# Middle down group as merged units: seven products for tiles 0 and 1 with tile 2's plain products, weight sums on GpSimd

## The chip, the cores and the metric

The kernel runs on one core of a Trainium2 chip. The metric is device time in microseconds; the run takes one execution of the program, from inputs in HBM to outputs in HBM. Everything is float32; the matmuls take float32 operands that were split into a high part (written as fp32r) and a low part, with three passes per product (high x high, high x low, low x high).

## The reference

One inference step of a hybrid decoder layer on 1024 prompt tokens and 8 sample tokens (1032 columns): RMSNorm, an input projection, three parallel head groups (sliding window attention, a gated linear recurrence, a short convolution), an output projection, and a feed-forward part. The change touches the last of these:

```python
up = rmsnorm(x, g_ffn) @ w_up
upc, ffn_buf_new = causal_conv(ffn_buf, up, ffn_conv_w)
u, gt = jnp.split(upc, 2, axis=-1)
x = x + (jax.nn.silu(gt) * u) @ w_down        # FF = 2816 -> D_MODEL = 1024
```

and the final RMSNorm over the 1024 features of `x`.

## The kernel before, in words

Features lie on the 128 partitions, tokens in the free dimension. The 1032 tokens are three tiles of 344 columns. The down projection contracts over 22 blocks of 128 features, taken as 11 pairs (`NG`), into 8 output blocks. The 11 pairs are three groups of 4, 3 and 4 (`GROUP_PAIRS`), so a matrix product of a group has 4, 3 or 4 chunks, each of three matmuls 128x128 by 128x344.

In a group the two features of a pair (index c, operand halves a11/a21 against a12/a22) and two output blocks (index i) form a 2x2 block product with tiles 0 and 1. Two forms exist.

- **Units** (`S_UNITS`, `s_product`): one unit is two output blocks for tiles 0 and 1 by seven products instead of eight (a Strassen-Winograd scheme). The weights come as a11, a12, a22 and the sums S1 to S4 (`unit_sums`, line 2287); the inputs as b11, b21, b22 and the differences D1 to D4, which were made once for a pair of features (`pair_diffs`) and stored in DRAM (`act_d`). Products run in the order p1, p5, p6, p2, p7, p3, p4 (`S_ORDER`) into three PSUM banks. p6 begins on a bank that ScalarE has filled with the negative of p1 (`preload`). p7 adds to the bank of p6 and waits for VectorE's read of it (`s_read`), p3 waits in the same way for the read of p5, p4 for the read of p7.
- **Plain pairs** (`T_PAIRS`): `t_pair` is tile 2 alone, `mid_pair` (line 2942) all three tiles, for two output blocks, with whole-weight splits (`t_hi`, `t_lo`).

TensorE's order of the down stage is: four plain pairs of tile 2 for group 0; four units of group 0 (`FIRST_S`, units 0 to 3); the middle group, four `mid_pair` with 8 products for tiles 0 and 1 and 4 for tile 2; four units of group 2 (`LAST_S`, units 8 to 11); four plain pairs of tile 2 for group 2. `MIXED` names the pairs of features that get differences; pairs 4 to 6 of the middle group did not.

Work around it. ScalarE makes the high parts (`s_hi`, `item_hi`), VectorE the low parts (`s_lo`, `item_lo`), the sums of the weights and all reads of PSUM into `x_sb`. Split weights lie in eight homes (`PART_HOME`, `home_free` says which product frees one), the raw weights in four buffers, the sums in four. The inputs of a group come from DRAM as *items* (`X_ITEMS`): each operand in two pieces, of chunks 0 and 1 (688 columns) and of the rest (688, in the middle group 344). Items pass through five staging places (`stage_of`), so a piece is loaded only after the piece five before it was split. The sync queue (SP) issues all loads in an order written by hand: `load_down(q)` for the weights, waiting for the splits of the load four before it, and after it as many `load_item` as the table `more` says. ScalarE, VectorE and TensorE too run orders that are written out by hand in the loops `for f in range(2)`. GpSimd carries the two boundary columns and the sample states through the up stage, then waits for the end and multiplies `x_sb` by the final factor (line 1032).

## Time and profile before

| what | value |
|---|---|
| median of 3 runs | 1041.6 us (1041.48 to 1042.73) |
| profiled execution | 1041.18 us |
| its span | 1039.4 us |
| mean granted TensorE clock | 0.997 |
| TensorE matmul busy | 1024.7 us (99%), 7426 instructions |
| VectorE busy | 786.1 us (76%) |
| ScalarE busy | 548.6 us (53%) |
| GpSimd busy | 66.0 us (6%) |
| down stage | 793.5 to 1029.6 us, of which the middle group 876.7 to 944.7 |

Times are from the start of the span. Each row of the profile names the line of the kernel, the engine, the operation, and its output and inputs by the program's names. A value in brackets behind a row is the idle time before it and what ended it. Rows are those of one execution; the span is 1.8 us shorter than that execution's time.

### The profile page before, as it was taken

How to read it: one execution, taken by the hardware profiler on the slowest of the kernel's cores; microseconds unless marked ns; L12 is line 12 of the kernel's file. 1: busy time of each engine (PE TensorE's matmuls, PEld its weight loads, DVE VectorE, ACT ScalarE, POOL GpSimd, SP SyncE). 2: the span in 40 equal slices, each digit the busy share in tenths (PEclk: the TensorE clock that was granted, in tenths of full speed). 3: DMA queues.
4: the chain of work that ended last, by engine and by line, in shares of the span. 5: the costliest groups of instructions: out<-in, count | busy, mean ns of one | idle time of the engine just before them, and what ended most of it. 6: DMA issues, size and time to landing. Idle time of an engine off the chain costs nothing.

```text
span 1039.4 us, 19531 instructions
## 1 busy us (share of the span) xinstructions
PE 1024.7 (99%) x7426; PEld 997.3 (96%) x7426; DVE 786.1 (76%) x1401; ACT 548.6 (53%) x1054; POOL 66.0 (6%) x161
## 2 busy tenths in 40 slices
PE   7999999999999999999999999999999999999996
PEld 7999988888999999999999999999999999999996
DVE  6754559888778899887886777687787896448964
ACT  7455444556545466555555555555556745125744
POOL 0100000000000011110100010010100000000023
PEclk9999999999999999999999999999999999999998
DMA  7211201021742312232132132122336976415354
GB/s 270 100 41 47 102 22 40 23 82 55 249 139 94 119 41 96 66 127 102 42 143 83 42 111 93 42 103 82 117 136 199 331 228 180 137 55 150 88 185 150
DMA packets 63293, 117.21 MB, mean 113 GB/s; under 512 B 5312, under 2 KB 46912, under 8 KB 63168
## 3 DMA queue, kind: packets, MB, share of 16 engines
q1 hardware_dynamic: 59376, 109.99, 31.5%
q10 hardware_dynamic: 3824, 5.96, 1.6%
q8 instruction: 60, 0.98, 0.4%
q14 instruction: 33, 0.27, 0.1%
HBM read 91.03 MB, written 25.95 MB: 113 GB/s over the span
## 4 chain that ended last, share of the span: by engine, by line
PE 98%; DMA 1%; DVE 0%; ACT 0%; SPq 0%; DVEq 0%; issue 0%
PE psum L2909 41%; PE psum L2986 10%; PE psum L2649 9%; PE psum L2859 9%; PE psum L2961 7%; PE psum L2938 6%; PE psum L2716 2%; PE psum L2683 2%; PE psum L2718 2%; PE psum L2877 2%; PE psum L2717 2%; PE psum L2793 2%; PE psum L2753 1%; PE psum L2803 1%; PE psum L2741 1%; DMA x_sb<-in_x 1%
## 5 line engine op out<-in xcount | busy, mean ns | idle before, releaser
L2909 PE MATMUL psum<-diff,w_hi 128*128 128x258 f32 x588 | 116.5, 283 | 0.0
L2909 PE MATMUL psum<-h_hi,w_lo 128*128 128x258 f32 x336 | 95.2, 283 | 0.0
L2909 PE MATMUL psum<-h_hi,w_hi 128*128 128x258 f32 x336 | 95.0, 283 | 0.0
L2909 PE MATMUL psum<-diff,w_lo 128*128 128x258 f32 x336 | 94.9, 282 | 0.0
L2909 PE MATMUL psum<-h_lo,w_hi 128*128 128x258 f32 x336 | 94.8, 282 | 0.0
L2909 PE MATMUL psum<-h_hi,act_lo 128*128 128x258 f32 x336 | 94.7, 282 | 0.0
L2909 PE MATMUL psum<-h_lo,act_hi 128*128 128x258 f32 x336 | 94.5, 281 | 0.0
L2909 PE MATMUL psum<-h_hi,act_hi 128*128 128x258 f32 x336 | 94.5, 281 | 0.0
L2909 PEld LDWEIGHTS psum<-diff,w_hi 128*128 128x128 f32 x588 | 94.0, 190 | 0.0
L2909 PEld LDWEIGHTS psum<-h_hi,w_hi 128*128 128x128 f32 x336 | 63.8, 190 | 0.0
L2909 PEld LDWEIGHTS psum<-diff,w_lo 128*128 128x128 f32 x336 | 63.6, 189 | 0.0
L2909 PEld LDWEIGHTS psum<-h_lo,w_hi 128*128 128x128 f32 x336 | 63.5, 189 | 0.0
L2909 PEld LDWEIGHTS psum<-h_hi,w_lo 128*128 128x128 f32 x336 | 63.4, 189 | 0.0
L2909 PEld LDWEIGHTS psum<-h_lo,act_hi 128*128 128x128 f32 x336 | 63.3, 188 | 0.0
L2909 PEld LDWEIGHTS psum<-h_hi,act_lo 128*128 128x128 f32 x336 | 63.2, 188 | 0.0
L2909 PEld LDWEIGHTS psum<-h_hi,act_hi 128*128 128x128 f32 x336 | 63.2, 188 | 0.0
L2909 PE MATMUL psum<-diff,act_hi 128*128 128x258 f32 x336 | 62.4, 283 | 0.0
L2239 DVE TENSOR_TENSOR x_sb<-psum,att 128x258 f32<-128x258 f32 x42 | 17.7, 425 | 58.7 <-PE psum L2909 57.9
L2909 PEld LDWEIGHTS psum<-diff,act_hi 128*128 128x128 f32 x336 | 52.4, 190 | 0.0
L2909 PE MATMUL psum<-diff,act_lo 128*128 128x258 f32 x168 | 47.6, 283 | 0.0
L2649 PE MATMUL psum<-h_hi,w_hi 128*128 128x344 f32 x144 | 47.0, 326 | 0.0
L2649 PE MATMUL psum<-h_hi,w_lo 128*128 128x344 f32 x144 | 46.0, 319 | 0.0
(404 smaller groups left out, 3312.0 us busy)
## 6 DMA issues: line engine op xcount, KB each, us to landing
raw<-in_w SPq DMA_DIRECT2D x76, 512.0 KB, 4.0
zb<-act_d SPq DMA_DIRECT2D x31, 344.0 KB, 4.9
att<-in_w SPq DMA_DIRECT2D x15, 512.0 KB, 4.9
act_d<-x_sb SPq DMA_DIRECT2D x7, 1032.0 KB, 5.0
raw<-in_w SPq DMA_DIRECT2D x18, 384.0 KB, 3.6
act_d<-att SPq DMA_DIRECT2D x10, 516.0 KB, 2.8
x_sb<-in_x SPq DMA_DIRECT2D x8, 516.0 KB, 4.8
x_d<-x_sb ACTq DMA_DIRECT2D x12, 344.0 KB, 2.5
```

The lines of the kernel that those rows point to most:

```text
L2649: ins = mm(out, a, b, start=(at == 0), stop=(at == n - 1))
L2683: ins = mm(first_ps[f], a, b[:, k, tile(t)], start=(at == 0), stop=(at == 3 * KD - 1))
L2716: mm(out, wh, h_hi[:, k, tile(t)], start=(k == 0), stop=False)
L2717: mm(out, wh, h_lo[:, k, tile(t)], start=False, stop=False)
L2718: ins = mm(out, wl, h_hi[:, k, tile(t)], start=False, stop=(k == KD - 1))
L2793: ins = mm(score_ps[:, 2 * g + c, low:], q_sb[rows, 2 * half_ + c, n * WIN:(n + 1) * WIN], k_sb[rows, (n - 1) * WIN + low:(n + 1) * WIN], ...
L2859: ins = mm(out, a, b, start=(at == 0), stop=(at == 3 * KD - 1))
L2877: ins = mm(first_bank[to], a, b, start=(c == k == p == 0), stop=(c == 1 and k == HALF - 1 and p == 2))
L2909: ins = mm(bank[to, q], a, b, start=(fresh and k == p == 0), stop=(k == HALF - 1 and p == 2), skip_group_check=True)
L2938: ins = mm(down_ps[T_BANKS[tp][i]], a, b, start=(c == k == q == 0), stop=(c == 1 and k == n - 1 and q == 2), skip_group_check=True)
L2961: ins = mm(down_ps[mid_banks(tp, t)[i]], a, b, start=(c == k == q == 0), stop=(c == 1 and k == n - 1 and q == 2), skip_group_check=True)
L2986: ins = mm(down_ps[S_BANKS[u % 2][b]], a, c, start=(p in ("p1", "p5") and k == q == 0), stop=(k == n - 1 and q == 2), skip_group_check=True)
```

## The change

- `MIXED` becomes all eleven pairs, so pairs 4 to 6 get differences and store them.
- The four middle pairs become merged units 4 to 7 (`MID_UNITS`): the seven products for tiles 0 and 1, and two products of tile 2, m0 and m1 (`mid_product`), which take the unsplit parts a11, a12 and a21, a22. The order on TensorE is p1, p5, p6, p2, m0, p7, p3, p4, m1 (`MID_ORDER`). A merged unit has eight split parts in eight homes (`MID_PARTS`, `MID_HOMES`).
- The inputs of the middle group are nine operands in 18 pieces instead of six in 12 (`MID_X`), in other places; those of the last group come in another order (`LAST_X`).
- The sums of the weights, of units 1 to 11, are made on GpSimd; unit 0's stay on VectorE. GpSimd also makes the low parts of b22 and D4 of the last group (`POOL_ITEMS`). A raw weight buffer is loaded again only when the sums that read it are done (the new wait in `load_down`).
- The hand-written orders of ScalarE, VectorE and the sync queue follow.

```diff
-MIXED = (0, 1, 2, 3, 7, 8, 9, 10)
+MIXED = tuple(range(NG))
...
-MID_PAIRS, END_PAIRS = T_PAIRS[1], T_PAIRS[2]
+MID_UNITS, END_PAIRS = T_PAIRS[1], T_PAIRS[2]
 DOWN_BANK = (3, 5, 2, 7, 1, 4, 6, 0)
-T_BANKS = ((3, 5), (2, 7), (1, 4), (6, 0)) + 4 * ((), ) + ((3, 5), (6, 0), (7, 1), (3, 5))
-MID_BANKS = ((3, 5), (6, 0), (7, 1))
+T_BANKS = ((3, 5), (2, 7), (1, 4), (6, 0)) + 4 * ((6, 0), ) + ((3, 5), (6, 0), (7, 1), (3, 5))
...
+MID_PARTS = S_PARTS + ("a21", )
+MID_ORDER = ("p1", "p5", "p6", "p2", "m0", "p7", "p3", "p4", "m1")
+MID_HOMES = ({"a11": 7, "S1": 0, "S2": 1}, {"a11": 0, "S1": 1, "S2": 7}, {"a11": 1, "S1": 7, "S2": 0}, {"a11": 7, "S1": 0, "S2": 1})
...
+def mid_step(u, step):
+    return ("T", u, step) if step[0] == "m" else ("S", u, step)
...
+def part_home(u, part):
+
+
+    if u in MID_UNITS:
+        return {"a12": 2, "S3": 3, "S4": 4, "a22": 5, "a21": 6, **MID_HOMES[u - MID_UNITS[0]]}[part]
+    return S_PARTS.index(part)
+
+
...
+MID_X = ("b11", "D1", "D2", "b21") + T_X + ("D3", "b22", "D4")
+LAST_X = ("D1", "D2", "b11", "b21", "D3", "b22", "D4")
+X_ITEMS = x_items(0, T_X) + x_items(0, S_X) + x_items(1, MID_X) + x_items(2, LAST_X) + x_items(2, T_X)
 X_N = numbered(X_ITEMS)
+POOL_ITEMS = x_items(2, ("b22", "D4"))
+ITEM_N = {**numbered([x for x in X_ITEMS if x not in POOL_ITEMS]), **numbered(POOL_ITEMS)}
+UNIT_SUMS = (("S1", "a21", "a22"), ("S2", "a11", "S1"), ("S3", "a11", "a21"), ("S4", "a12", "S2"))
...
                     old, o, oc = LOADS[q - 4]
-                    sp.wait_ge(down_lo, SPLIT_N[(old, o, oc) if old == "T" else ("S", o, ("a11", "a22")[oc])])
+                    sp.wait_ge(down_lo, SPLIT_N[(old, o, oc) if old == "T" else ("S", o, ("a21" if o in MID_UNITS else "a11", "a22")[oc])])
+                    if old == "S":
+                        sp.wait_ge(down_sum_ready, len(SUMS) * o + SUMS.index(("S3", "S4")[oc]) + 1)
...
-                more = {("S", 0): (1, 1), ("S", 1): (1, 1), ("S", 2): (2, 2), ("S", 3): (1, 2), ("T", 4): (2, 2), ("T", 5): (2, 1),
-                        ("T", 6): (2, 2), ("T", 7): (1, 3), ("S", 8): (1, 1), ("S", 9): (1, 1)}.get((kind, u), (0, 0))[c]
+                more = {("S", 0): (1, 1), ("S", 1): (1, 1), ("S", 2): (2, 2), ("S", 3): (1, 7), ("S", 4): (1, 1), ("S", 5): (2, 3),
+                        ("S", 7): (0, 9), ("S", 8): (1, 1), ("S", 9): (1, 1)}.get((kind, u), (0, 0))[c]
                 for _ in range(more):
...
+            def unit_sums(u):
+
+                for c in range(2):
+                    s = down_slot("S", u, c)
+                    pool.wait_ge(raw_landed[raw_of(s)], landed_at(s))
+                for name, a, b in UNIT_SUMS:
+                    pool.wait_ge(down_lo, SPLIT_N["S", u - 1, name])
+                    if b in SUMS:
+                        pool.wait_ge(down_sum_ready, len(SUMS) * u + SUMS.index(b) + 1)
+                    right = by_chunk(unit_sum(u, b)) if b in SUMS else unit_block(u, b)
+                    nc.gpsimd.tensor_tensor(by_chunk(unit_sum(u, name)), unit_block(u, a), right, ALU.add).then_inc(down_sum_ready, 1)
+
+            for u in range(1, LAST_S[-1] + 1):
+                unit_sums(u)
+                if u == LAST_S[0]:
+                    for item in POOL_ITEMS:
+                        pool.wait_ge(act_hi_ready, X_N[item])
+                        nc.gpsimd.tensor_tensor(item_home(y_lo, item), item_stage(item), f32(item_home(y_hi, item)), ALU.subtract).then_inc(pool_split, 1)
...
+                    for u in MID_UNITS:
+                        s_hi(u, "a22")
+                        s_hi(u, "a21")
+                        preload(u)
+                        if u == MID_UNITS[0]:
+                            item = X_N[1, "D4", 0] - 1
+                            item_hi(item)
+                            item_hi(item + 1)
+                        if u < MID_UNITS[-1]:
+                            for part in ("a11", "S1", "S2", "a12", "S3", "S4"):
+                                s_hi(u + 1, part)
+                            continue
+                        nc.scalar.preload_act_table_set(LN_EXP)
+                        item, u = X_N[2, LAST_X[0], 0] - 1, LAST_S[0]
+                        item_hi(item)
+                        item_hi(item + 1)
+                        s_hi(u, "a11")
+                        item_hi(item + 2)
+                        item_hi(item + 3)
+                        s_hi(u, "S1")
+                        for n in range(4, 8):
+                            item_hi(item + n)
+                        s_hi(u, "S2")
+                        s_hi(u, "a12")
...
+                    if p == HALF - 1 and not fin:
+                        item = X_N[1, "D2", 0] - 1
+                        for k, (q, part) in enumerate((("p5", "a11"), ("p6", "S1"), ("p2", "S2"), ("p7", "a12"))):
+                            s_lo(u + 1, part)
+                            s_read(u, q)
+                            item_lo(item + 2 * k)
+                            item_lo(item + 2 * k + 1)
+                        s_lo(u + 1, "S3")
+                        s_read(u, "p3")
+                        s_lo(u + 1, "S4")
+                        for n in range(item + 8, item + 12):
+                            item_lo(n)
+                        continue
...
+                    for u in MID_UNITS:
+                        s_lo(u, "a22")
+                        s_lo(u, "a21")
+                        if u == MID_UNITS[0]:
+                            item = X_N[1, "D4", 0] - 1
+                            item_lo(item)
+                            item_lo(item + 1)
+                        s_read(u, "p5")
+                        if u < MID_UNITS[-1]:
+                            s_read(u, "p6")
+                            s_lo(u + 1, "a11")
+                            s_lo(u + 1, "S1")
+                            s_read(u, "p2")
+                            mid_read(u, 0)
+                            s_lo(u + 1, "S2")
+                            s_lo(u + 1, "a12")
+                            s_read(u, "p7")
+                            s_lo(u + 1, "S3")
+                            s_read(u, "p3")
+                            s_lo(u + 1, "S4")
+                            s_read(u, "p4")
+                            mid_read(u, 1)
+                            continue
+                        item = X_N[2, LAST_X[0], 0] - 1
+                        item_lo(item)
+                        item_lo(item + 1)
+                        s_read(u, "p6")
+                        s_lo(u + 1, "a11")
+                        item_lo(item + 2)
+                        item_lo(item + 3)
+                        s_lo(u + 1, "S1")
+                        item_lo(item + 4)
+                        s_read(u, "p2")
+                        for n in range(5, 8):
+                            item_lo(item + n)
+                        mid_read(u, 0)
+                        s_lo(u + 1, "S2")
+                        s_read(u, "p7")
+                        s_lo(u + 1, "a12")
+                        item_lo(item + 8)
+                        item_lo(item + 9)
+                        s_read(u, "p3")
+                        s_lo(u + 1, "S3")
+                        s_read(u, "p4")
+                        mid_read(u, 1)
+                        s_lo(u + 1, "S4")
...
+            def mid_product(u, i):
+
+                pe.wait_ge(down_lo, SPLIT_N["S", u, ("a12", "a21")[i]])
+                if u == MID_UNITS[0]:
+                    item_wait(pe, (1, "t2b", 1))
+                    pe.wait_ge(t_copied, 7 + i)
+                else:
+                    pe.wait_ge(down_read, BANK_FREE["T", u, i])
+                n = chunks_of("S", u)
+                for c in range(2):
+                    part, x = f"a{i + 1}{c + 1}", T_X[c]
+                    wh_, wl_ = unit_home(split_hi, u, part), unit_home(split_lo, u, part)
+                    for k in range(n):
+                        cols = slice(k * P, (k + 1) * P)
+                        wh, wl, xh, xl = wh_[:, cols], wl_[:, cols], y_hi[1][x][:, k, :], y_lo[1][x][:, k, :]
+                        for q, (a, b) in enumerate(((wh, xh), (wh, xl), (wl, xh))):
+                            ins = mm(down_ps[T_BANKS[u][i]], a, b, start=(c == k == q == 0), stop=(c == 1 and k == n - 1 and q == 2),
+                                     skip_group_check=True)
+                ins.then_inc(down_done, 1)
...
-            for tp in MID_PAIRS:
-                mid_pair(tp)
+            for u in MID_UNITS:
+                for step in MID_ORDER:
+                    if step[0] == "m":
+                        mid_product(u, int(step[1]))
+                    else:
+                        s_product(u, step)
...
```

Three places of the orders written out by hand. In these rows `L2336` is `item_lo`, `L2348` `s_read`, `L2369` `mid_read`, `L2317` and `L2319` `s_lo`, `L2310` `t_lo` of the changed kernel (`L2305`, `L2317`, `L2340`, `L2282`, `L2284`, `L2275` before).

VectorE at the end of unit 3, before, from the read of p7 on: whole-weight splits and pieces of the middle group's operands between the reads of p3 and p4, then the first two mid reads.

```order
L2317 TENSOR_TENSOR x_sb<-x_sb,psum 128x344 [waits down_read,x2_back3,down_done]
L2275 TENSOR_TENSOR w_lo1<-raw0,w_hi1 128x768 [waits down_hi]
L2305 TENSOR_TENSOR h_lo<-zb,h_hi 128x2x344 [waits act_hi_ready]
L2305 TENSOR_TENSOR h_lo<-pad_u,h_hi 128x344 [waits act_hi_ready]
L2317 TENSOR_TENSOR x_sb<-x_sb,psum 128x344 [waits down_read,x2_back3,down_done]
L2305 TENSOR_TENSOR h_lo<-zb,h_hi 128x2x344 [waits act_hi_ready]
L2305 TENSOR_TENSOR h_lo<-zb,h_hi 128x344 [waits act_hi_ready]
L2317 TENSOR_TENSOR x_sb<-x_sb,psum 128x344 [waits x2_back3,down_done]
L2275 TENSOR_TENSOR act_lo0<-raw1,act_hi0 128x768 [waits down_hi]
L2340 TENSOR_TENSOR x_sb<-x_sb,psum 128x344 [waits t_copied,down_done] x2
```

The same place now, from the read of p3 on: S4 of unit 4, the pieces of D3 and b22, the read of p4, a22 and a21 of unit 4, D4's two pieces, and (x2) the reads of p5 and p6 of unit 4.

```order
L2348 TENSOR_TENSOR x_sb<-x_sb,psum 128x344 [waits down_read,x2_back3,down_done]
L2317 TENSOR_TENSOR act_lo0<-att,act_hi0 128x384 [waits down_hi]
L2336 TENSOR_TENSOR hy_lo_50<-zb,hy_hi_49 128x688 [waits act_hi_ready]
L2336 TENSOR_TENSOR hy_lo_50<-zb,hy_hi_49 128x344 [waits act_hi_ready]
L2336 TENSOR_TENSOR h_lo<-pad_u,h_hi 128x2x344 [waits act_hi_ready]
L2336 TENSOR_TENSOR h_lo<-zb,h_hi 128x344 [waits act_hi_ready]
L2348 TENSOR_TENSOR x_sb<-x_sb,psum 128x344 [waits x2_back3,down_done]
L2319 TENSOR_TENSOR act_lo0<-raw0,act_hi0 128x384 [waits down_hi]
L2319 TENSOR_TENSOR act_lo1<-raw2,act_hi1 128x384 [waits down_hi]
L2336 TENSOR_TENSOR h_lo<-zb,h_hi 128x2x344 [waits act_hi_ready]
L2336 TENSOR_TENSOR h_lo<-zb,h_hi 128x344 [waits act_hi_ready]
L2348 TENSOR_TENSOR x_sb<-x_sb,psum 128x344 [waits down_done] x2
```

Before, the pieces that were still to come were followed by reads of the mid pairs; now the reads of unit 4's p5 and p6 stand behind D4's pieces.

The sync queue from the second weight load of unit 5 (`att`) on, now: seven pieces of items (27 to 33), the first weight load of unit 6 (`raw2`), D4's first piece, the second load of unit 6, D4's second piece.

```order
L813 DMA att<-in_w 128x3x256 [waits down_sum_ready,down_lo]
L857 DMA pad_u<-act_d 128x344 [waits act_stored,act_split]
L857 DMA zb<-act_d 128x2x344 [waits act_stored,act_split]
L857 DMA zb<-act_d 128x344 [waits act_stored,act_split]
L857 DMA zb<-act_d 128x2x344 [waits act_stored,act_split]
L857 DMA zb<-act_d 128x344 [waits act_stored,act_split]
L857 DMA pad_u<-act_d 128x2x344 [waits act_stored,act_split]
L857 DMA zb<-act_d 128x344 [waits act_stored,act_split]
L813 DMA raw2<-in_w 128x3x256 [waits down_sum_ready,down_lo]
L857 DMA zb<-act_d 128x2x344 [waits act_stored,act_split]
L813 DMA raw0<-in_w 128x3x256 [waits down_sum_ready,down_lo]
L857 DMA zb<-act_d 128x344 [waits act_stored,act_split]
```

Before, the loads and the pieces alternated there.

```order
L807 DMA att<-in_w 128x3x256 [waits down_lo]
L851 DMA pad_u<-act_d 128x344 [waits act_stored,act_split]
L851 DMA zb<-act_d 128x2x344 [waits act_stored,act_split]
L807 DMA raw2<-in_w 128x3x256 [waits down_lo]
L851 DMA zb<-act_d 128x344 [waits act_stored,act_split]
L851 DMA zb<-act_d 128x2x344 [waits act_stored,act_split]
L807 DMA raw0<-in_w 128x3x256 [waits down_lo]
L851 DMA zb<-act_d 128x2x344 [waits act_stored,act_split]
L851 DMA pad_u<-act_d 128x2x344 [waits act_stored,act_split]
```

D4's first piece has moved behind a weight load that waits for `down_lo`, here for the low part of a21 of unit 4, and for `down_sum_ready`.

VectorE in unit 7, now, from the first weight part of unit 8 (a11) on: D2's two pieces, S1, one piece of b11, the read of p2, three pieces, the read of m0, S2, the read of p7, a12. Ahead of the first row stand the read of p5, D1's two pieces and the read of p6.

```order
L2319 TENSOR_TENSOR w_lo0<-raw2,w_hi0 128x512 [waits down_hi]
L2336 TENSOR_TENSOR h_lo<-zb,h_hi 128x2x344 [waits act_hi_ready] x2
L2317 TENSOR_TENSOR w_lo0<-att,w_hi0 128x512 [waits down_hi]
L2336 TENSOR_TENSOR hy_lo_50<-zb,hy_hi_49 128x688 [waits act_hi_ready]
L2348 TENSOR_TENSOR x_sb<-x_sb,psum 128x344 [waits down_done]
L2336 TENSOR_TENSOR hy_lo_50<-zb,hy_hi_49 128x688 [waits act_hi_ready]
L2336 TENSOR_TENSOR hy_lo_50<-pad_u,hy_hi_49 128x688 [waits act_hi_ready]
L2336 TENSOR_TENSOR hy_lo_50<-zb,hy_hi_49 128x688 [waits act_hi_ready]
L2369 TENSOR_TENSOR x_sb<-x_sb,psum 128x344 [waits t_copied,down_done]
L2317 TENSOR_TENSOR w_lo1<-att,w_hi1 128x512 [waits down_hi]
L2348 TENSOR_TENSOR x_sb<-x_sb,psum 128x344 [waits down_read,down_done]
L2319 TENSOR_TENSOR w_lo1<-raw0,w_hi1 128x512 [waits down_hi]
```

Before, the last pieces of the same operands stood between pairs of mid reads, behind four sums and four splits for unit 8.

```order
L2284 TENSOR_TENSOR w_lo0<-raw2,w_hi0 128x512 [waits down_hi]
L2282 TENSOR_TENSOR w_lo0<-att,w_hi0 128x512 [waits down_hi]
L2282 TENSOR_TENSOR w_lo1<-att,w_hi1 128x512 [waits down_hi]
L2284 TENSOR_TENSOR w_lo1<-raw0,w_hi1 128x512 [waits down_hi]
L2340 TENSOR_TENSOR x_sb<-x_sb,psum 128x344 [waits down_done] x2
L2305 TENSOR_TENSOR hy_lo_50<-zb,hy_hi_49 128x688 [waits act_hi_ready]
L2305 TENSOR_TENSOR hy_lo_50<-pad_u,hy_hi_49 128x688 [waits act_hi_ready]
L2305 TENSOR_TENSOR hy_lo_50<-zb,hy_hi_49 128x688 [waits act_hi_ready] x2
L2340 TENSOR_TENSOR x_sb<-x_sb,psum 128x344 [waits down_done] x2
```

The read of p7 of unit 7, for which p4 waits on TensorE, now has all pieces of D1, D2, b11 and b21 ahead of it.

## Rows read from the trace of the kernel before

**Rows 1.** Page, part 1: busy us, share and instructions of each engine.

```profile
PE 1024.7 (99%) x7426; PEld 997.3 (96%) x7426; DVE 786.1 (76%) x1401; ACT 548.6 (53%) x1054; POOL 66.0 (6%) x161
```

**Rows 2.** Chain that ended last: start us, us, engine, output, line, count.

```profile
371.00 422.68 PE psum L2909 x3528
...
823.78 52.90 PE psum L2986 x336
876.68 68.01 PE psum L2961 x432
```

**Rows 3.** Windows: us, busy (count) of PE, PEld, DVE, ACT, POOL; PEclk, DMA.

```profile
863.30:876.50 13.20, 13.20 (x86) 13.20 (x85) 9.14 (x15) 7.66 (x13) 0.00 (x0) 1.00 0.62 192
876.50:944.50 68.00, 68.00 (x434) 68.00 (x433) 34.67 (x55) 19.46 (x27) 0.00 (x0) 1.00 0.42 129
```

**Rows 4.** Timeline of VectorE, units 2, 3 and mid: start us, us, operation.

```profile
858.53 0.69 DVE L2284 TENSOR_TENSOR w_lo<-att,w_hi 128x512 fp32r<-128x512 f32 x1 [0.15 <-ACT w_hi L1401]
...
867.30 0.51 DVE L2317 TENSOR_TENSOR x_sb<-x_sb,psum 128x344 f32<-128x344 f32 x1 [2.43 <-PE psum L2986]
...
871.50 1.29 DVE L2305 TENSOR_TENSOR hy_lo<-zb,hy_hi 128x688 fp32r<-128x688 f32 x2
...
931.33 1.28 DVE L2282 TENSOR_TENSOR w_lo<-att,w_hi 128x512 fp32r<-128x512 f32 x2
...
933.14 0.93 DVE L2340 TENSOR_TENSOR x_sb<-x_sb,psum 128x344 f32<-128x344 f32 x2
...
935.89 1.65 DVE L2305 TENSOR_TENSOR hy_lo<-zb,hy_hi 128x688 fp32r<-128x688 f32 x2
```

**Rows 5.** Timeline of the sync queue and of ScalarE, 864 to 912.

```profile
864.90 0.37 SPq L807 DMA_DIRECT2D att<-in_w  x1
...
874.97 0.37 SPq L807 DMA_DIRECT2D raw<-in_w  x1
875.76 0.36 SPq L851 DMA_DIRECT2D zb<-act_d  x1
...
880.09 0.78 ACT L1419 ACTIVATE hy_hi<-zb 128x688 fp32r<-128x688 f32 x1 [1.75 <-DMA zb<-act_d]
...
911.65 1.28 ACT L1637 ACT_TABLE_LOAD   x1
```

**Rows 6.** Timeline of GpSimd and VectorE, where both run.

```profile
27.91 2.41 POOL L997 TENSOR_TENSOR act_lo<-raw,act_hi 128x1024 fp32r<-128x1024 f32 x1 [25.65 <-DVE h_lo L1732]
...
1007.04 0.93 POOL L1032 TENSOR_TENSOR x_sb<-x_sb,zb 128x344 f32<-128x344 f32 x1 [212.30 <-ACT zb L1670]
1007.88 1.23 DVE L2275 TENSOR_TENSOR w_lo<-raw,w_hi 128x1024 fp32r<-128x1024 f32 x1 [1.68 <-ACT w_hi L1389]
1007.93 1.96 POOL L1032 TENSOR_TENSOR x_sb<-x_sb,zb 128x344 f32<-128x344 f32 x1
1009.02 0.50 DVE L2360 TENSOR_TENSOR att<-att,psum 128x344 f32<-128x344 f32 x1
1009.59 1.39 DVE L2275 TENSOR_TENSOR w_lo<-raw,w_hi 128x1024 fp32r<-128x1024 f32 x1
...
1017.02 1.94 POOL L1032 TENSOR_TENSOR x_sb<-x_sb,zb 128x344 f32<-128x344 f32 x1
1018.09 1.25 DVE L2360 TENSOR_TENSOR att<-att,pad_u 128x344 f32<-128x344 f32 x1
...
1022.62 0.52 DVE L2360 TENSOR_TENSOR att<-att,pad_u 128x344 f32<-128x344 f32 x1 [0.56 <-ACT pad_u L1657]
```

**Rows 7.** TensorE's first matmuls, timeline, and two windows at the end.

```profile
6.57 0.62 PE L2683 MATMUL psum<-h_hi,w_hi 128*128 128x344 f32 x1 [6.57 <-DVE h_lo L1732]
...
12.54 0.49 PE L2683 MATMUL psum<-h_hi,w_hi 128*128 128x344 f32 x1
...
1032.00:1034.00 2.00, 0.00 (x0) 0.00 (x0) 1.33 (x2) 1.08 (x3) 0.00 (x0) 0.87 0.00 0
1034.00:1036.00 2.00, 0.00 (x0) 0.00 (x0) 1.90 (x3) 0.00 (x0) 0.00 (x0) 0.50 0.79 281
```

250 lines of the change are left out of this document (77 added, 173 removed).

## The prediction

> **What bounds the kernel now.** I read the shares of busy time first: TensorE is busy 99% of the span [rows 1]. So only fewer or faster matmuls, or new gaps between them, move the end. The chain that ended last, in order of time, is TensorE's own work from 371 us on and says that the first down group and the middle group run without a break: 336 matmuls in 52.90 us and 432 in 68.01 us, 0.1574 us each in both [rows 2]. The busy times by stretch show what stands beside it: VectorE is busy 9.14 of 13.20 us in unit 3 and only 34.67 of 68.00 us in the middle group, GpSimd not at all [rows 3]. So the middle group has slack on VectorE, but that is a mean over 68 us. What counts is where the new work stands in VectorE's order, and what TensorE waits for behind it.
>
> **The change, part by part.** The profiled execution took 1041.2 us (span 1039.4), the median of the runs is 1041.6; the sum is made against 1041.2, and 0.4 is added at the end.
>
> *Removed matmuls.* Tiles 0 and 1 go from eight plain products a unit to seven. Four units x one product x 3 chunks x 3 passes = 36 matmuls, the same 36 by which TensorE's order is shorter. 36 x 0.1574 = **5.7 us less**. It lies on the path, if TensorE stays packed.
>
> *Pairs 4 to 6 get differences* (four 344-wide subtractions each, and 516 KB more to store). The other eight pairs do this already, in the up stage, which TensorE goes through in one piece of 3528 matmuls [rows 2]; the new ones stand at the same place between the same steps. Cost nothing; if the cover were gone, twelve 344-wide operations at 0.52 us [rows 6] are 6 us.
>
> *From unit 3 into unit 4.* Unit 3 starts at 863.3 (the middle group's begin at 876.5 [rows 3] less 84 x 0.1574). VectorE reads its first bank (p5) at 867.30 [rows 4]; from here it has, by its new order and before it comes to unit 4's own reads: five more reads plus this one at 0.43 (two back to back take 0.93), seven weight splits of 384 columns and six pairs of input splits. Two 512-wide splits take 1.28, so one comes every 0.60 us, a 344-wide operation every 0.43; between them lie 0.47 for 384 columns. Two pieces, 688 and 344 wide, take 1.29 and come 1.22 apart [rows 4]. 6 x 0.43 + 7 x 0.47 + 6 x 1.22 = 13.2, so a21 of unit 4 is split at **880.5** with no wait at all in between. Before, whole pair splits and four pairs of input splits stood there, and nothing of TensorE's hung on their end.
>
> Behind this stands a wait that I take for the main one. The sync queue issues the load of D4's first piece only after the load for unit 6, and that one waits for the split of a21. VectorE's next instructions are the splits of D4, and only then the reads of p5 and p6 of unit 4, for which p7 waits on TensorE. In the trace of before the same sequence (weight load at 874.97, piece at 875.76, split on ScalarE at 880.09) takes 5.1 us [rows 5]. Then 0.78 for the split on ScalarE, 0.15 for the hand-over [rows 4], 1.22 for both on VectorE and 0.94 for two reads: the read of p6 is done 8.3 us after a21's split. The load is the loose part: three more pieces are under way, 3.3 to 5.5 us for the 4.3 from the piece's issue.
>
> *GpSimd's sums.* A GpSimd operation on two tensors takes 0.93 us at 344 columns and 2.41 at 1024 [rows 6], so 1.02 at 384 and 1.30 at 512, against 0.60 on VectorE. Does it hold VectorE up? VectorE's addition of two SBUF tensors took 1.25 us while GpSimd's operation that began at 1017.02 ran to 1018.96, and 0.52 without one; the reverse shows in that GpSimd operation, 1.94 instead of 0.93 behind a VectorE split. An addition with a PSUM operand took 0.50 beside a running GpSimd operation [rows 6]. So the reads are free, and each split waits for the rest of a running sum: 0.73 us longer for 0.87 of overlap. The sums of unit 5 are released by the splits of S1, S2, S3 and S4 of unit 4 and its weights are long landed (issued at 864.90 [rows 5]), so all four fall into the stretch above. Three begin beside a read (1.02 + 0.15 - 0.43 = 0.75 held up each), the fourth beside a split (1.0). That is 3.2 us: a21's split moves to **883.8**. Ends: nothing, if they happen to lie beside waits, and 4.1. On the way the read of p7 of unit 3 comes at 875.6, where p4 would start at 874.6: **1.0 us** of stall. Unit 4 then starts at 877.6, its sixth product would start at 886.1, and the read of p6 is done at 883.8 + 8.3 = 892.1: **6.0 us** of stall. Behind it four splits and two reads stand before p7's read is through, 4 x 0.47 + 3 x 0.43 = 3.2 us and up to 0.3 of a running sum, for 2.8 us of matmuls: **0.5 us**.
> The row of the 1009.59 split speaks for less: 1.39 instead of the 1.23 of the one at 1007.88, with 0.3 us of overlap (the GpSimd operation that began at 1007.93 ran to 1009.89) [rows 6]. The Trainium skill (SBUF — State Buffer, "SBUF: two separate sides") has it that the pair of ports is a lock held for the whole instruction, the loser blocked fully. Going by 1009.59 the four sums would cost 1.9 us and not 3.2, and the kernel 1.3 less; by the rule it would be 3.4. I stay with 0.73 in 0.87, the longest overlap that the trace has.
> The Trainium skill also speaks against the move itself: GPSIMD Engine Reference, "Engine selection", leaves elementwise work on whole tiles to VectorE, with GpSimd about two times slower; 1.30 against 0.60 agrees. By its figure for 2048 columns (4497 ns), an estimate from that page, a 384-wide sum would be 0.84 us, and the kernel 0.7 us faster than by the rows.
>
> *The clock.* With TensorE idle at the end the granted clock falls: 0.87 in the stretch to 1034, 0.50 after it, which is the 1.2 GHz level [rows 7]. What a fall costs: at the start, behind idle time, the first 19 matmuls begin between 6.57 and 12.54 [rows 7], 5.97 us for 18 steps that take 2.83 at 0.1574, the 2.4 GHz level; some 0.7 of the 3.1 us more are waits for input, which leaves 2.4. Ends 0 and 2.4 for the first stall, which is the longest by far; I take **1.9**, since slow matmuls cover the 0.5 above.
>
> *Steady units 5 and 6.* The tightest place is p4 behind the read of p7: four instructions from m0's end (read, two splits, read) end 2.2 us later, at 2.8 p4 starts. No cost.
>
> *Unit 7 into unit 8.* Times from unit 7's start. ScalarE: p1 done at 1.42, preload (344 wide, 0.4) to 2.0, table load 1.28 [rows 5], first split of D1 to 4.05; VectorE starts D1 at 4.2. Before it comes to the read of p7 it has four pairs of 688-wide splits (1.65 for two, 1.58 apart), three 512-wide weight splits and four reads [rows 4]: 6.3 + 1.8 + 1.7 = 9.8, so the read ends at 14.0 to 14.2. TensorE would start p4 at 11.33: **2.9 us** of stall; 2.6 if no load is late, 4 if b21's second piece is 1 us late. Before, these splits stood between reads that nothing on TensorE waited for so soon. GpSimd's sums for unit 8 fall into unit 6 and cost nothing here. Its four input splits (688 wide, 1.7 each) and the sums of unit 9 may hold VectorE up in unit 8; p7 has 0.3 us to spare there: 0 to 1.5, I take 0.
>
> *First and last group.* VectorE loses four sums a unit (2.4 us) and is held up by at most 5.2 us of GpSimd's, mostly beside its waits and reads. Unit 1 is tightest: a11's split ends about 1 us before TensorE needs it. 0 to 1 us; I take 0.
>
> **Sum:** -5.7 + 1.0 + 6.0 + 0.5 + 1.9 + 2.9 = +6.6; 1041.2 + 6.6 = 1047.8, and against the median 1048.2. **Forecast 1048**, slower by 0.6%.
>
> **Rivals.**
> *The stalls without their surroundings.* GpSimd's sums miss the tight stretch and the clock stays up. Then a21 is split at 880.5, p6's read is done at 887.8 to 888.8 against 885.0, and unit 7 keeps its stall: -5.7 + 3.3 + 0.4 + 2.8 = +0.8, 1042.4. For it: the sums' places rest on hand-overs of 0.15 us. Against it: they are released by just these splits.
> *TensorE stays packed.* One mechanism: VectorE's reads of p6 in unit 4 and of p7 in unit 7 are in time, because its splits take less than I count or D4's piece is there at once. It decides at 885.0 for the one and 11.3 us into unit 7 for the other; then the 36 matmuls are all that is left: 1041.6 - 5.7 = 1036, faster by 0.5%. For it: VectorE has 33 us idle in the middle group [rows 3]. Against it: 13.2 us of work would have to go into 9.4, and no row for a split is shorter than I took.
> *More than forecast.* The 2.9 us stall brings the clock down too (2.4), unit 8's p7 and unit 1 wait (1 each): 1048 + 4.4 = 1052.4. For it: the clock has fallen within the stretches right behind the last matmul [rows 7]. Against it: 2.9 us is half of the first stall.
>
> **How the numbers follow.** Forecast 0.58, the first rival 0.18, packed 0.08, more than forecast 0.16. Within 0.2% (2.1 us, about what a measurement of this kernel can tell from no change) lies the first rival, but for 0.01 of its spread, 0.17; faster is the packed case, 0.08; slower the rest, 0.75. The range leaves out the packed case and the far half of the last: it begins at the first rival's lower ends, -5.7 + 2.8 + 0.3 + 2.7 = +0.1 or 1041.7, and ends with the last, 1052.5.
>
> **What would show it.** TensorE's waits, of which there are none now: one of 5 to 6 us ahead of p7 of unit 4 released by VectorE's read, about 1 us ahead of p4 of unit 3, 2.9 us ahead of p4 of unit 7, none in units 5 and 6; matmuls at half the pace behind the first, with a granted clock under 1; the middle stage at 62.3 us of matmuls plus these; GpSimd at 44 sums with means over 1.0 us; VectorE's splits in unit 3 at 1.2 to 1.5 us where a sum runs. Wrong if p6's read of unit 4 is not behind D4, if D4's piece was issued before a21's split, or if splits beside GpSimd keep their 0.5 to 0.8 us.

## The result and the profile after

The changed kernel takes **1053.1 us** (median of 6 runs, 1051.9 to 1055.9) against 1041.5 for the kernel before in the same comparison: ratio 1.0118, 95% interval 1.0108 to 1.0129, slower by 12 us. Forecast were 1048 in a range of 1041.7 to 1052.5. The direction was right; the size was not, and the time lies above the range. The profiled execution has a span of 1052.3 us, 12.9 more than before.

The page, part 1, answers to [rows 1]; under it the waits of TensorE from 800 to 1000 us (what waited, for what: us in total, times, longest).

```profile
PE 1025.0 (97%) x7390; PEld 996.0 (95%) x7390; DVE 815.4 (77%) x1419; ACT 562.1 (53%) x1088; POOL 133.1 (13%) x209
```

```profile
PE psum L3018 <- DVE x_sb L2348: 12.6, 4, 5.5
```

TensorE has 36 matmuls less (7390 for 7426) and is busy for 97% of the span instead of 99%. Four waits, all for VectorE's reads (`L2348` is `s_read`), make 12.6 us where there was none. VectorE and ScalarE are fuller, and GpSimd has the 44 sums and four input splits.

The four waits and what follows two of them, in TensorE's timeline (start us, us, operation; in brackets the idle time before it and what ended it; `L3018` is `s_product`):

```profile
847.21 0.40 PE L3018 MATMUL psum<-hy_hi,act_hi 128*128 128x344 f32 x1 [2.39 <-DVE x_sb L2348]
...
878.54 0.39 PE L3018 MATMUL psum<-h_hi,act_hi 128*128 128x344 f32 x1 [0.89 <-DVE x_sb L2348]
...
894.84 0.63 PE L3018 MATMUL psum<-hy_hi,w_hi 128*128 128x344 f32 x1 [5.51 <-DVE x_sb L2348]
895.27 0.49 PE L3018 MATMUL psum<-hy_lo,w_hi 128*128 128x344 f32 x1
...
951.42 0.40 PE L3018 MATMUL psum<-h_hi,act_hi 128*128 128x344 f32 x1 [3.81 <-DVE x_sb L2348]
```

They stand ahead of p7 of unit 1, p4 of unit 3, p7 of unit 4 and p4 of unit 7. The busy times by stretch (us; busy and count of PE, PEld, DVE, ACT, POOL; granted clock; DMA) answer to [rows 3, 7]:

```profile
863.00:876.50 13.50, 13.50 (x88) 13.50 (x87) 12.74 (x19) 8.34 (x17) 4.85 (x5) 1.00 0.55 157
876.50:950.00 73.50, 64.65 (x389) 63.45 (x387) 47.33 (x80) 27.86 (x52) 16.61 (x14) 0.95 0.39 121
894.00:901.00 7.00, 6.16 (x22) 6.19 (x23) 5.40 (x12) 2.00 (x5) 3.26 (x3) 0.53 0.02 5
951.00:956.00 5.00, 4.58 (x19) 4.62 (x20) 4.93 (x7) 3.15 (x6) 3.45 (x2) 0.66 0.78 245
```

In unit 3 VectorE is busy for 12.74 of 13.50 us where it was for 9.14 of 13.20. The granted clock is 0.53 in the seven us from the third wait on, and 0.66 in the five from the fourth: TensorE, idle before both, ran matmuls at the 1.2 GHz level, 0.287 us apart instead of 0.157.

**Where the time went.** Each stretch's steps against 0.1574 us a matmul, that is wait, restart (what the first two steps behind a wait take beyond the wait and 0.1574 each, 0.24 us) and slow matmuls together, in the profiled execution:

| place | wait | slow matmuls | lost in all |
|---|---|---|---|
| p7 of unit 1 | 2.39 | 0 | 2.63 |
| p4 of unit 3 | 0.89 | 0 | 1.13 |
| p7 of unit 4 | 5.51 | 19 | 8.37 |
| p4 of unit 7 | 3.81 | 11 | 5.55 |
| three gaps under 0.3 (units 4, 5, 10) | | 0 | 0.72 |
| start of the down stage (793.80 for 793.51) | | | 0.29 |
| 36 matmuls fewer | | | -5.7 |

The sum is 13.0, against 12.9 between the spans.

**Ahead of p7 of unit 4.** VectorE from unit 3's first read to unit 4's p5 and p6 (`L2336` is `item_lo`, `L2317` and `L2319` are `s_lo`), then the sync queue and ScalarE:

```profile
870.14 0.51 DVE L2348 TENSOR_TENSOR x_sb<-x_sb,psum 128x344 f32<-128x344 f32 x1 [0.43 <-PE psum L3018]
...
872.67 2.11 DVE L2336 TENSOR_TENSOR hy_lo<-zb,hy_hi 128x688 fp32r<-128x688 f32 x2
...
875.60 1.48 DVE L2336 TENSOR_TENSOR h_lo<-zb,h_hi 128x688 fp32r<-128x688 f32 x1
...
880.43 1.17 DVE L2317 TENSOR_TENSOR act_lo<-att,act_hi 128x384 fp32r<-128x384 f32 x1
881.51 2.12 DVE L2336 TENSOR_TENSOR hy_lo<-zb,hy_hi 128x688 fp32r<-128x688 f32 x2
...
885.19 1.01 DVE L2319 TENSOR_TENSOR act_lo<-raw,act_hi 128x384 fp32r<-128x384 f32 x2
892.05 0.88 DVE L2336 TENSOR_TENSOR h_lo<-zb,h_hi 128x688 fp32r<-128x688 f32 x1 [5.85 <-ACT h_hi L1443]
...
893.77 0.93 DVE L2348 TENSOR_TENSOR x_sb<-x_sb,psum 128x344 f32<-128x344 f32 x2
```

```profile
886.23 0.37 SPq L813 DMA_DIRECT2D raw<-in_w  x1
886.70 0.44 SPq L857 DMA_DIRECT2D zb<-act_d  x1
```

```profile
891.25 0.78 ACT L1443 ACTIVATE h_hi<-zb 128x688 fp32r<-128x688 f32 x1 [7.98 <-DMA zb<-act_d]
```

From the first read (870.14) to the end of a21's split (a22 and a21 are the two of 885.19, done at 886.20) VectorE never waits, and takes 16.1 us. Pairs of splits take 2.11 and 2.12 instead of 1.29 [rows 4]. Only then is D4's first piece issued (886.70), behind the weight load that waited for a21. It is split on ScalarE at 891.25, on VectorE at 892.05, and the two reads end 8.5 us after a21's split (forecast 8.3). In between VectorE idles for 5.85.

**In unit 1**, which the prediction had at 0 to 1 us, GpSimd makes eight sums (`L1044`) of units 1 and 2 between 830 and 845, and VectorE seven splits of unit 1:

```profile
833.97 1.50 DVE L2319 TENSOR_TENSOR w_lo<-raw,w_hi 128x512 fp32r<-128x512 f32 x1
835.39 2.38 DVE L2317 TENSOR_TENSOR w_lo<-att,w_hi 128x512 fp32r<-128x512 f32 x2
837.69 1.77 DVE L2319 TENSOR_TENSOR w_lo<-att,w_hi 128x512 fp32r<-128x512 f32 x1
839.38 1.78 DVE L2317 TENSOR_TENSOR act_lo<-att,act_hi 128x512 fp32r<-128x512 f32 x1
841.09 0.50 DVE L2348 TENSOR_TENSOR x_sb<-x_sb,psum 128x344 f32<-128x344 f32 x1
841.51 1.58 DVE L2317 TENSOR_TENSOR act_lo<-att,act_hi 128x512 fp32r<-128x512 f32 x1
```

```profile
830.37 3.29 POOL L1044 TENSOR_TENSOR att<-raw,att 128x512 f32<-128x512 f32 x2 [35.34 <-DMA att<-in_w]
833.62 1.30 POOL L1044 TENSOR_TENSOR att<-raw 128x512 f32<-128x512 f32 x1
834.88 1.74 POOL L1044 TENSOR_TENSOR att<-att 128x512 f32<-128x512 f32 x1
837.34 1.58 POOL L1044 TENSOR_TENSOR att<-raw 128x512 f32<-128x512 f32 x1 [0.72 <-DVE w_lo L2317]
839.06 1.56 POOL L1044 TENSOR_TENSOR att<-raw,att 128x512 f32<-128x512 f32 x1
```

A 512-wide split comes every 0.60 us alone [rows 4]. Here the seven take 10.1 us instead of 4.2, most of them behind a running sum of 1.30 (the sums too stretch, to 1.56 to 1.74). The reads keep their 0.50. All 5.9 us of hold-up stand before the reads of p5 and p6 of unit 1, for which p7 waits. The read of p6, before and now:

```profile
843.71 0.50 DVE L2317 TENSOR_TENSOR x_sb<-x_sb,psum 128x344 f32<-128x344 f32 x1
```

```profile
846.57 0.50 DVE L2348 TENSOR_TENSOR x_sb<-x_sb,psum 128x344 f32<-128x344 f32 x1
```

Before, it ended at 844.21, only 0.2 us ahead of p7 of unit 1 (844.37); now it ends 2.9 us later. The eight sums took 5.1 us on VectorE before, but that is not what was won. Unit 2's four, 2.5 us, stood in this same stretch. Unit 1's four stood ahead of it, and without them VectorE comes to the seven splits only 0.5 us earlier (833.97 for 834.49): it was 0.6 us later than before already, one more split was held up by 0.7 us, and it waited 0.6 us for TensorE ahead of the read of 833.54. So 5.9 - 2.5 - 0.5 = 2.9. GpSimd could not begin unit 1's sums before 830.37, when their weights had landed, and so the sums of two units fell into one.

**Ahead of p4 of unit 7** the read of p7 (`950.76`) is late. ScalarE waited for b11's second piece, which was issued at 941.16, when D1's first piece had been split, and landed 5.1 us later; VectorE, behind it, idled for 0.80 us:

```profile
946.32 0.78 ACT L1443 ACTIVATE hy_hi<-zb 128x688 fp32r<-128x688 f32 x1 [2.37 <-DMA zb<-act_d]
```

```profile
947.13 0.88 DVE L2336 TENSOR_TENSOR hy_lo<-zb,hy_hi 128x688 fp32r<-128x688 f32 x1 [0.80 <-ACT hy_hi L1443]
...
950.76 0.51 DVE L2348 TENSOR_TENSOR x_sb<-x_sb,psum 128x344 f32<-128x344 f32 x1
```

### The profile page after: what moved, and what is told of

It reads as the page before. It is cut to its first block, busy times and chain, and to the rows that moved or that the text cites. A ratio compares the mean times of both kernels' runs of the same rounds, so it can differ in the third digit from the quotient of the medians.

```text
span 1052.3 us, 19681 instructions
## 1 busy us (share of the span) xinstructions
PE 1025.0 (97%) x7390; PEld 996.0 (95%) x7390; DVE 815.4 (77%) x1419; ACT 562.1 (53%) x1088; POOL 133.1 (13%) x209
## 4 chain that ended last, share of the span: by engine, by line
PE 94%; DVE 2%; DMA 1%; issue 1%; ACT 0%; SPq 0%; DVEq 0%; ACTq 0%
PE psum L2944 40%; PE psum L3018 12%; PE psum L2684 9%; PE psum L2894 9%; PE psum L2973 6%; PE psum L2718 2%; PE psum L2751 2%; PE psum L2753 2%; PE psum L2912 2%; PE psum L2752 2%; PE psum L2994 2%; PE psum L2828 2%; PE psum L2788 1%; PE psum L2838 1%; PE psum L2776 1%
## 5 line engine op out<-in xcount | busy, mean ns | idle before, releaser
L2348 DVE TENSOR_TENSOR x_sb<-x_sb,psum 128x344 f32<-128x344 f32 x72 | 36.3, 505 | 15.1 <-PE psum L3018 14.9
```

The costliest lines, as they stand in the source:

```text
L2348: V.tensor_tensor(y, y, src, ALU.subtract if p in ("p5", "p6") else ALU.add).then_inc(down_read, 1)
```

## The experiments

Each run was timed beside the kernel before on one chip; ratios are those of this and before, and microseconds are worked out from them at 1041. On that scale the changed kernel is +12.3.

### The new differences alone

```diff
-MIXED = (0, 1, 2, 3, 7, 8, 9, 10)
+MIXED = tuple(range(NG))
```

> The kernel before with the differences of pairs 4 to 6 alone (what the middle group reads as b12 is then the difference that is stored in its place; nothing else differs). Theory A: these twelve subtractions and the larger stores lie beside TensorE's 3528 matmuls: 1041.5, within 0.3 us. Theory B: they are part of what the change costs: 2 to 6 us more, and the down stage starts later by as much.

This kernel leaves out what the middle group needs of b12 and serves for its time alone.

Measured: 1040.97 us, ratio 0.9998 (0.9988 to 1.0007). The differences cost nothing that shows, to within 1 us either way, as forecast. The profiled execution, at 1042.40 the slowest of the ten, loses 1.3 us in unit 0; since the median does not move, that is not put down to them.

### D4 issued earlier

Two entries of the table `more`:

```diff
-("S", 3): (1, 7), ("S", 4): (1, 1)
+("S", 3): (1, 9), ("S", 4): (0, 0)
```

> The changed kernel (1053.1 us) with one move on the sync queue: both pieces of D4 of the middle group are issued ahead of the weight load that waits for the split of a21, not behind it. Theory A (the queue): the 5.5 us wait ahead of p7 of unit 4 is that load's latency. D4 has then landed before a21 is split at 886.2; VectorE splits both pieces (1.22) and reads p5 and p6 (0.93) by 888.4, and p7 could start at 889.0: the wait goes, and the 20 slow matmuls behind it (2.6) with it, 1053.1 - 5.5 - 2.6 = 1045.0. Theory B (VectorE's load): VectorE has more in front of these reads than fits, whatever the transfer does: the wait shrinks to 2 to 3 us, the clock falls all the same, about 1050.

Measured: 1046.7 us, ratio 1.0047 (1.0029 to 1.0064), that is 7.4 us less than the changed kernel. VectorE at the same place:

```profile
884.39 1.01 DVE L2319 TENSOR_TENSOR act_lo<-raw,act_hi 128x384 fp32r<-128x384 f32 x2
885.33 1.29 DVE L2336 TENSOR_TENSOR h_lo<-zb,h_hi 128x688 fp32r<-128x688 f32 x2
886.54 0.92 DVE L2348 TENSOR_TENSOR x_sb<-x_sb,psum 128x344 f32<-128x344 f32 x2
```

D4's splits follow a21's at once, the two reads end 2.1 us behind it, and the wait ahead of p7 of unit 4 with its slow matmuls is gone (8.4 us in the table above). Two numbers in the order of a queue carried most of the loss. About 1 us came back in unit 7 (lost there 6.5 instead of 5.6: 4.16 of wait and 15 slow matmuls), 0.5 ahead of p6 of unit 4 and 0.6 in unit 8. Theory A.

### GpSimd's sums: three ways to take them off

First all of them back to VectorE:

```diff
-            for u in range(1, LAST_S[-1] + 1):
-                unit_sums(u)
...
+                            if u == MID_UNITS[0]:
+                                unit_sums(u + 1)
...
+                            unit_sums(u + 2)
...
```

> The changed kernel with all weight sums back on VectorE (units 2 to 4 as in the kernel before, unit 5 behind the reads of p5 and p6 of unit 4, units 6 to 8 at the end of the unit two before them). GpSimd keeps four input splits. Theory A (GpSimd's sums hold VectorE's splits up for the rest of their run): the 2.4 us wait in unit 1 goes although VectorE has 2.4 us more to do there; in unit 3 four hold-ups of 0.6 to 0.9 go and four sums of 0.47 come, so a21's split is 1.3 us nearer and the wait ahead of p7 of unit 4 is 4.2 instead of 5.5: 1053.1 - 2.4 - 1.3, less 0 to 0.9 for p4 of unit 3, 1048.5 to 1049.4. Splits on VectorE take 0.6 us (512 wide) throughout. Theory B (the hold-ups lie in idle time, and GpSimd takes work off VectorE): VectorE is 2.4 us a unit fuller and every wait is longer, 1055 or more.

Measured: 1051.2 us, ratio 1.0083 (1.0060 to 1.0107), 3.6 us less. The waits in units 1 and 3 went, and that ahead of p7 of unit 4 was 3.88 with 12 slow matmuls. But the one ahead of p4 of unit 7 doubled, to 7.47: the weight loads of the last group's unit and a late input piece went out together, and ScalarE waited 6.0 us for the piece. Theory A holds in three places, but the time is above its 1048.5 to 1049.4; neither theory had the fourth place.

Then those of units 1 to 3 alone:

```diff
+                        if u < 3:
+                            unit_sums(u + 1)
                         s_lo(u + 1, "a11")
                         s_read(u, "p5")
...
```

> The changed kernel with the weight sums of units 1 to 3 back on VectorE, at the places of the kernel before; those of units 4 to 11 stay on GpSimd. Theory A (GpSimd's sums of units 1 and 2 hold up seven splits in a row in the stretch from 833 to 845 us, 1.5 to 2.4 us each where they take 0.6): the 2.4 us wait ahead of p7 of unit 1 goes, although VectorE has 2.4 us more to do: 1053.1 - 2.4 = 1050.7; the waits in units 3, 4 and 7 stay as they are within 0.5. Theory B (the wait is VectorE's amount of work): it stays or grows, 1053 to 1055.

Measured: 1051.06 us, ratio 1.0085 (1.0069 to 1.0100), 3.4 us less; the wait in unit 1 is gone. That is 2.4 us; in the profiled execution another 1.2 went in unit 4, where the wait ahead of p7 was 4.75 us. VectorE from 833 to 845, by form (busy us, mean ns):

```profile
L2333 DVE TENSOR_TENSOR att<-raw,att 128x512 f32<-128x512 f32 x4 | 2.8, 689 | 0.1
...
L2317 DVE TENSOR_TENSOR w_lo<-att,w_hi 128x512 fp32r<-128x512 f32 x3 | 2.0, 682 | 0.0
...
L2317 DVE TENSOR_TENSOR act_lo<-att,act_hi 128x512 fp32r<-128x512 f32 x2 | 1.4, 680 | 0.0
```

With eight sums more to do (`L2333`, 0.68 each) VectorE is in time, since its splits take 0.68 again and not 1.2 to 1.8 (the 2.38 above is for two). So the wait came from the two engines' running beside each other, not from the amount of work. Theory A.

Third, VectorE untouched, and GpSimd's sums of unit 5 held back:

```diff
             def unit_sums(u):
 
+                if u == MID_UNITS[1]:
+                    pool.wait_ge(down_read, READ_N["S", u - 1, "p6"])
```

> The changed kernel with one added wait on GpSimd: its four sums for unit 5 begin only when VectorE has read p6 of unit 4. VectorE's work and order are untouched. Theory A (these four sums hold VectorE's splits up by 3.2 us in unit 3): the splits of unit 3 take 0.5 (384 wide) and 1.2 us (a pair) again, the 0.9 us wait ahead of p4 of unit 3 goes, and a21 of unit 4 is split 3.2 us earlier against a unit that ends 0.9 earlier, so the wait ahead of p7 of unit 4 falls from 5.5 to 3.2: 1053.1 - 0.9 - 2.3 = 1049.9, and 0 to 1 less for fewer slow matmuls. Theory B (the hold-ups lie in time in which VectorE would wait for late pieces anyway): both waits stay within 0.5, 1053.

Measured: 1053.07 us, ratio 1.0109 (1.0095 to 1.0123). Unit 3 of this run:

```profile
870.66 0.51 DVE L2350 TENSOR_TENSOR x_sb<-x_sb,psum 128x344 f32<-128x344 f32 x1 [0.43 <-PE psum L3020]
...
873.20 1.29 DVE L2338 TENSOR_TENSOR hy_lo<-zb,hy_hi 128x688 fp32r<-128x688 f32 x2
...
875.30 0.87 DVE L2338 TENSOR_TENSOR h_lo<-zb,h_hi 128x688 fp32r<-128x688 f32 x1
...
879.98 1.29 DVE L2338 TENSOR_TENSOR hy_lo<-zb,hy_hi 128x688 fp32r<-128x688 f32 x2
...
882.83 1.02 DVE L2321 TENSOR_TENSOR act_lo<-raw,act_hi 128x384 fp32r<-128x384 f32 x2
```

```profile
892.45 0.62 PE L3020 MATMUL psum<-hy_hi,w_hi 128*128 128x344 f32 x1 [3.73 <-DVE x_sb L2350]
```

The pairs of splits take 1.29 again. From the first read to a21's split pass 13.2 us, to the tenth what the prediction had without hold-ups, instead of 16.1: the four sums cost **2.9 us** there (forecast 3.2). The wait in unit 3 is gone, that ahead of p7 of unit 4 is 3.73 for 5.51. Yet the time did not move by anything that shows: the interval overlaps that of the changed kernel. In the profiled execution 3.3 us were gained at the two places, and 0.8 lost ahead of p4 of unit 4, 0.7 in unit 10, and 1.7 in unit 1, where a wait of 2.58 us was followed by slow matmuls. The mechanism is as theory A has it, the time as theory B; alone the edit is worth next to nothing.

### Unit 7, and what comes behind it

```diff
                         s_read(u, "p2")
+                        mid_read(u, 0)
+                        s_read(u, "p7")
                         for n in range(5, 8):
                             item_lo(item + n)
-                        mid_read(u, 0)
                         s_lo(u + 1, "S2")
-                        s_read(u, "p7")
```

> The changed kernel with one move on VectorE in unit 7: the reads of m0 and p7 come ahead of three input splits (second piece of b11, both of b21) and of the split of S2, not behind them. Theory A (the order): the 3.8 us wait ahead of p4 of unit 7 and the slow matmuls behind it (1.5) are these four splits and the late piece before the read: both go, 1053.1 - 5.3 = 1047.8. Theory B (too much work): the splits are then late for p1, p5 and p6 of unit 8, TensorE waits there instead, and the time stays within 1 us of 1053. The wait ahead of p7 of unit 4 is as before in both.

Measured: 1053.26 us, ratio 1.0117 (1.0093 to 1.0141): nothing. Theory B has the place and the time, but not the reason. The wait ahead of p4 of unit 7 is gone, and this one stands ahead of p6 of unit 8 (TensorE, then ScalarE; `L1443` splits inputs, `L1450` is `preload`):

```profile
959.05 0.40 PE L3018 MATMUL psum<-h_hi,w_hi 128*128 128x344 f32 x1 [2.90 <-ACT psum L1450]
```

```profile
956.75 0.78 ACT L1443 ACTIVATE h_hi<-zb 128x688 fp32r<-128x688 f32 x1 [1.71 <-DMA zb<-act_d]
957.43 0.61 ACT L1421 ACTIVATE act_hi<-att 128x512 fp32r<-128x512 f32 x1
957.95 0.61 ACT L1425 ACTIVATE act_hi<-raw 128x512 fp32r<-128x512 f32 x1
958.47 0.44 ACT L1450 ACTIVATE psum<-psum 128x344 f32<-128x344 f32 x1
```

ScalarE stood before D4's last piece, with the preload behind it. With 12 slow matmuls this costs 4.7 us for the 5.6 that went in unit 7, and in this profile unit 1's wait (2.65) was followed by slow matmuls too, 1.8 more. The wait in unit 7 had covered the one in unit 8. So the preload was moved too:

```diff
-                        for n in range(10, 14):
+                        for n in range(10, 12):
                             item_hi(item + n)
...
                     preload(u)
+                    if u == LAST_S[0]:
+                        for i in range(2):
+                            item_hi(X_N[2, "D4", i] - 1)
```

> The changed kernel with the order of the run on unit 7 (reads of m0 and p7 ahead of three input splits and S2's) and one more move: ScalarE makes the preload for p6 of unit 8 ahead of the two splits of D4, not behind them. In the run with the first move alone the wait ahead of p4 of unit 7 went and one of 2.9 us came ahead of p6 of unit 8, for a preload that stood behind the last D4 piece's landing on ScalarE. Theory A (a single late piece in ScalarE's order): that wait goes too, and with it the slow matmuls: 1053.1 - 3.8 - 1.5 = 1047.8, up to 0.5 more. Theory B (the last group's fourteen inputs simply take this long through five buffers): TensorE waits for another of them, D3, b22 or D4, in unit 8, and the time stays within 1.5 us of 1053.

Measured: 1051.87 us, ratio 1.0105 (1.0091 to 1.0118). The wait ahead of p6 of unit 8 is gone, and 2.45 us with 12 slow matmuls stand ahead of p4 of unit 8, for VectorE's read of p7 there. The time is theory B's, the reason neither's. It is not an input on its way through the five buffers: the splits of unit 9's parts stood before that read, and waited for GpSimd's sums of unit 9, which it begins behind its four input splits.

### All of it, and the orders mended one by one

The edits together (D4 early, both of unit 7, sums of units 1 to 3 on VectorE, sums of unit 5 held):

> All four edits together: D4 of the middle group issued ahead of the weight load, VectorE's order in unit 7, ScalarE's preload ahead of the splits of D4, sums of units 1 to 3 on VectorE, GpSimd's sums of unit 5 held until p6 of unit 4 is read. If the waits and the clock behind them are the whole of what the change cost, the 36 matmuls are left: 1041.5 - 5.7 = 1035.8, and up to 1 us more for small waits (0.5 ahead of p6 of unit 4 for ScalarE's preload, 0.2 in unit 5): 1036 to 1037. If the waits feed on something else (transfers that collide once TensorE is faster), new ones come in units 4 and 8, and it stays above 1040.

Measured: 1042.73 us, ratio 1.0018 (1.0009 to 1.0027). From +12.3 to +1.9 us, with no slow matmul left in the profile, but not the 1036 to 1037 expected: 1.13 us ahead of p6 of unit 4 and 2.45 ahead of p4 of unit 8 remain. That profile is of the fastest of the eleven executions, 1040.8; what the other 2 us up to the median are, no trace shows. So for these two waits, VectorE's and ScalarE's orders were mended next:

```diff
                         for n in range(item + 8, item + 11):
                             item_hi(n)
+                        preload(u + 1)
+                        item_hi(item + 11)
...
-                        preload(u)
+                        if u > MID_UNITS[0]:
+                            preload(u)
...
                         s_lo(u + 1, "a11")
-                        s_lo(u + 1, "S1")
                         s_read(u, "p2")
-                        s_lo(u + 1, "S2")
                         s_read(u, "p7")
+                        s_lo(u + 1, "S1")
+                        s_lo(u + 1, "S2")
```

> The run with all edits (1042.7, its profile 1040.8) and two more moves for the two waits that its trace shows. VectorE in unit 8 reads p2 and p7 ahead of the splits of S1 and S2 of unit 9, whose sums GpSimd makes late, behind its four input splits: the 2.45 us wait ahead of p4 of unit 8 goes. ScalarE makes the preload for p6 of unit 4 ahead of the last piece of b22: the 1.1 us wait there goes. Theory A (single instructions in the wrong place): 1042.7 - 2.45 - 1.1 = 1039.1. Theory B (GpSimd's sums of unit 9 are late whatever VectorE does first): TensorE waits for S1 at p5 of unit 9 by 1 to 2 us instead, 1041 or more.

Measured: 1041.95 us, ratio 1.0013 (1.0004 to 1.0022). Both waits went, and 0.99 us came ahead of p4 of unit 4, where the held sums of unit 5 now run, 2.22 ahead of p6 of unit 9, and 1.03 in unit 0 in the profiled execution. It is theory B's time, with the wait one product later than it named. Against the run before it nothing is gained that shows: the intervals overlap widely.

With these orders, all sums were also put back on VectorE:

```diff
-            for u in range(4, LAST_S[-1] + 1):
-                unit_sums(u)
+            for u in (LAST_S[0],):
...
```

> The same orders with all weight sums on VectorE (GpSimd keeps four input splits). Theory A (with the orders mended GpSimd's sums buy nothing, and their hold-ups of VectorE cost what they save): the time is that of the run beside it within 1 us, 1038 to 1040, with splits of 0.6 us. Theory B (VectorE needs the relief): four more operations of 0.47 to 0.6 a unit make its reads late in units 3, 4 and 7 to 9, 1042 or more.

Measured: 1044.35 us, ratio 1.0035 (1.0022 to 1.0047). It has 3.96 us with 18 slow matmuls ahead of p7 of unit 8. So GpSimd's sums are not worthless: with the orders mended and none of them the kernel is 2.3 us slower (the two intervals just touch). What counts is which.

Then GpSimd's late sums alone went back:

```diff
             for u in range(4, LAST_S[-1] + 1):
-                unit_sums(u)
+                if u not in (MID_UNITS[1], LAST_S[1]):
+                    unit_sums(u)
...
```

> The run with all edits and mended orders (1042.0, its profile 1041.1), in which GpSimd makes the sums of units 4, 6, 7, 8, 10 and 11 and VectorE those of unit 9 (behind its reads of p2 and p7 of unit 8) and of unit 5 (behind its reads of p5 and p6 of unit 4); the hold of GpSimd's sums of unit 5 is gone with them. The trace of that run has 2.2 us ahead of p6 of unit 9 for ScalarE's preload, which stands behind sums of unit 9 that GpSimd began only after its input splits, 0.4 ahead of p7 of unit 8 and 1.0 ahead of p4 of unit 4, where the late sums of unit 5 hold VectorE up. Theory A (GpSimd's late sums): the 2.2 and the 1.0 go, 1042.0 - 3.2 = 1038.8. Theory B (VectorE cannot take four more sums in unit 8): p4 of unit 8 or p5 of unit 9 waits as long, 1041 or more.

Measured: 1041.18 us, ratio 1.0003 (0.9994 to 1.0012). 0.47 us is left ahead of p4 of unit 4, 0.64 ahead of p7 of unit 8, and 2.69 ahead of p6 of unit 9 with 12 slow matmuls. So theory A fails where it counted most: the sums of unit 9 are early and the preload of unit 9 is late all the same, behind a squaring on ScalarE that waits for the read of p3 (1.98 us idle, and 1.85 in the trace of the run with mended orders, whose wait had been put down to the sums). Theory B's places, p4 of unit 8 and p5 of unit 9, do not wait.

The last edit is for that squaring:

```diff
                         s_lo(u + 1, "S2")
+                        s_read(u, "p3")
                         s_lo(u + 1, "a12")
...
```

> The last run with one more move: VectorE reads p3 of unit 8 ahead of the splits of a12 and S3 of unit 9. In the trace of the last run TensorE waits 2.7 us ahead of p6 of unit 9 for ScalarE's preload, which stands behind a squaring that waits for that read, and the read behind two splits of 1.8 us beside GpSimd's sums; 11 slow matmuls (1.4) follow. Theory A: both go: 1041.2 - 2.7 - 1.0 = 1037.5, faster than the kernel before by 0.3%. Theory B (unit 9's splits are late as a whole): another wait of 1 us or more comes in unit 9, and the time is 1039.5 or more.

Measured: **1039.02 us** against 1040.58, ratio **0.9982** (0.9973 to 0.9992): faster than the kernel before by 0.2%. This is one comparison, and the last of a row in which each edit was chosen by the trace of the one before; the gain is no larger than the 2.1 us that the prediction took for what a measurement of this kernel can tell. The interval just misses that of the run before it (0.9994 to 1.0012). It lies between the theories: the wait ahead of p6 of unit 9 is down to 0.60, and 1.14 us stand ahead of p7 of unit 9, a wait as theory B has it. Its page, and its waits from 800 to 1000 us:

```profile
PE 1020.0 (98%) x7390; PEld 991.2 (96%) x7390; DVE 812.0 (78%) x1439; ACT 561.0 (54%) x1088; POOL 104.7 (10%) x189
```

```profile
PE psum L3035 <- DVE x_sb L2357: 2.1, 3, 1.1
PE psum L3035 <- ACT psum L1451: 0.6, 1, 0.6
```

Of the 5.7 us that the 36 matmuls are worth, 1.9 arrive. The losses left in the profiled execution, counted as in the table above, are 4.4: units 4 (0.7), 8 (0.7) and 9 (0.8 and 1.4) carry most of them. Whether they too can be ordered away was not tried.

## Why the prediction came out low

Step by step, in us:

| step | forecast | measured |
|---|---|---|
| 36 matmuls removed | -5.7 | -5.7 |
| differences | 0 | 0 (ratio 0.9998) |
| a21 of unit 4 split, from the first read | 13.2 + 3.2 | 13.2 + 2.9 |
| wait ahead of p4 of unit 3 | 1.0 | 0.89 |
| wait ahead of p7 of unit 4 | 6.0 | 5.51 |
| behind it | 0.5 | 0 |
| clock | 1.9, once | 2.6 and 1.5 |
| unit 5; unit 6 | 0 | 0.3; 0 |
| wait ahead of p4 of unit 7 | 2.9 | 3.81 |
| first group | 0 | 2.4 |
| last group | 0 | 0.3 (ahead of p6 of unit 10) |
| restarts behind waits, start of the stage | 0 | 0.24 each, 0.29 |

**Right:** the main wait, its place, its cause and its size, and the hold-up by GpSimd's sums in unit 3. The queue's order (D4 behind the weight load that waits for a21) was taken from the order of the instructions and the 8.3 us from four rows of before (its terms as they stand add up to 8.2); 8.5 were measured, and moving the two loads took it away.

**The step that failed** is "First and last group", with its "0 to 1 us; I take 0". It set at most 5.2 us of hold-up against waits and reads as a whole, where unit 3 had been gone through instruction by instruction, and it took a11's split, with 1 us to spare, for the tightest place. The tightest place was the read of p6 of unit 1, with 0.2 us to spare. Ahead of it eight sums of GpSimd ran, not four, those of unit 2 released one by one by just the splits that they held up: 5.9 us for seven splits, against 3.0 won by the sums taken off. The run with the sums of units 1 to 3 back on VectorE took this wait away. The 2.4 us would have made the forecast 1050.4.

**The second** is the clock, which was let fall once; "The 2.9 us stall brings the clock down too" was left to a rival of 0.16. It fell there, behind 3.8 us, and cost 1.5. The first fall cost 2.6, a bit more than the end of 2.4 taken from the start of the kernel. The remaining 0.9 is unit 7's wait, mis-sized: a piece landed late and VectorE idled 0.80 us for it. The prediction had such a case at its upper end, "4 if b21's second piece is 1 us late", but the late piece was b11's second. These three make 2.4 + 2.2 + 0.9 = 5.5. Unit 3 and 4 fell short by 1.1, and the restarts (four times 0.24), the start of the stage and the small gaps, which were not counted, add 2.0: 6.6 + 5.5 - 1.1 + 2.0 = 13.0, against 12.9 between the spans.

Of the rivals "more than forecast" came nearest, 1052.4, by two of the three mechanisms that it named: the second fall of the clock (2.4 there, 1.5 measured) and unit 1 (1 there, 2.4 measured). The third, a wait ahead of p7 of unit 8, did not come, so that its sum is so near is partly luck. "The stalls without their surroundings" is answered by the run with unit 5's sums held: without GpSimd's hold-up the wait ahead of p7 of unit 4 is 3.7 us, within its 2.8 to 3.8, but the clock fell all the same, which it had ruled out.

The Trainium skill's rule (SBUF — State Buffer, "SBUF: two separate sides") that the loser of the port is blocked fully is borne out: where a sum of 1.30 and a split of 0.60 alternated in unit 1, a split took 1.57 to 1.78, little less than the 1.9 of the two one after the other, and reads of PSUM stayed at 0.50. The advice of the Trainium skill to leave such work to VectorE (GPSIMD Engine Reference, "Engine selection") agrees with the run for units 1 to 3, 3.4 us faster with their sums on VectorE; the run with mended orders and no GpSimd sum, 2.3 us slower than its fellow, says that it doesn't hold for all of them here.

## What to carry to other kernels

Where two engines share a port, the work that is moved is not free beside the engine it was taken from: lay the moved operations beside the other engine's order one by one, at every place where they run and not at the tightest alone. When a wait goes, look at once for what it covered: four times here a removed wait was followed by a new one two to four products later, behind another engine. And a load that is urgent should not stand in an in-order queue behind one that waits for compute.

## What was not expected of the hardware

- The fall of the clock does not follow the length of the wait. Waits of 2.39, 2.45 and 2.22 us (the changed kernel's unit 1, the run with all edits, the one with the orders) left TensorE at 0.157 a matmul; waits of 2.45, 2.50, 2.58, 2.65 and 2.69 in other runs were followed by 11 or 12 matmuls at 0.287, two of them only 1.1 to 1.2 us after the wait. Each such fall costs about 1.5 us. Behind longer waits it was 2.6 after 5.51 us (19 slow matmuls), but 1.4 after 5.58 (9 slow, the run with both edits of unit 7), and 2.5 after 3.96 as after 7.47 (18 slow each, the two runs with all sums on VectorE). So 1 us less of waiting can be worth 2.5 us or nothing; in the run with unit 5's sums held, such a fall in unit 1 took back 1.5 us.
- The first two steps behind a wait lose 0.24 us on top of it, in the three waits of the changed kernel where no slow matmul follows at once.
- GpSimd's operations lengthen as VectorE's do: fourteen of the 512-wide sums average 1466 ns, and the shortest take 1.29.
